# Unread identity products in PE's waits, and shorter chains in the norms, the router and the two tails

## What is computed

```python
for l in range(2):
    x_lat = x_lat + mod_l[2] * mixer(...)                 # layer 0 also for x_ctx
    h = _modulate(_rmsnorm(x_lat, norm_ffn[l]), mod_l[3], mod_l[4])
    # layer 0: 512 tokens (latent and context), layer 1: 256
    y = _hier_moe(tokens, ...)   # group = argmax of 4, then top 2 of its 8 experts, gates from a softmax
    x_lat = x_lat + mod_l[5] * y
return _rmsnorm(x_lat, final_norm)
```

## Time and profile before

| | |
|---|---|
| runs | median 2405.39 us, 2403.98 to 2409.56 us, 3 runs |
| the profiled execution | 2406.93 us, its span 2405.6 us |
| PE busy | 2192.5 us, 91% of the span |
| DVE, ACT, POOL busy | 657.5, 357.0, 121.5 us |
| DMA | 601.75 MB, mean 250 GB/s |
| mean granted clock of PE | 0.959 of full |

### The profile page before, as it was taken

The page is one execution under the profiler, slowest core; times in us unless marked ns, Lnnn a source line. Parts: engine busy times, 40 slices in busy tenths (PEclk is TensorE's granted clock), DMA queues, the critical chain, the costliest instruction groups (busy, mean ns, idle before and its releaser), DMA issues. The chain is left out here.

```text
span 2405.6 us, 27733 instructions
## 1 busy us (share of the span) xinstructions
PE 2192.5 (91%) x11542; PEld 1348.4 (56%) x11542; DVE 657.5 (27%) x1485; ACT 357.0 (15%) x831; POOL 121.5 (5%) x164
## 2 busy tenths in 40 slices
PE   6987998899999986999979999998599999989998
PEld 2454664656665543444555554544376458858873
DVE  2142332422222212313531111111355231034201
ACT  2052431200000001112520000000121122011000
POOL 4000000010000001000000000000110000000000
PEclk9988999899999998899989999999799999999999
DMA  9453163599999997621189999999644432443441
GB/s 331 143 216 136 56 260 149 209 414 420 420 420 420 421 420 295 225 71 67 50 322 415 420 419 420 419 420 418 229 142 134 133 112 97 158 140 119 153 152 41
DMA packets 154309, 601.75 MB, mean 250 GB/s; under 512 B 15289, under 2 KB 19073, under 8 KB 103488
## 3 DMA queue, kind: packets, MB, share of 16 engines
q1 hardware_dynamic: 144512, 582.98, 62.9%
q0 software_dynamic: 8144, 11.57, 1.5%
q10 hardware_dynamic: 1520, 5.32, 0.6%
HBM read 589.84 MB, written 21.23 MB: 254 GB/s over the span
## 5 line engine op out<-in xcount | busy, mean ns | idle before, releaser
L366 PE MATMUL psum<-ring,h_t 128*128 128x512 f32 (+1 forms) x1024 | 430.3, 582 | 4.5 <-ACT h_t L1072 2.1
L366 PEld LDWEIGHTS psum<-ring,h_t 128*128 128x128 f32 x1024 | 192.9, 193 | 234.8 <-issue 230.4
L399 PE MATMUL psum<-h_t,ring 128*128 128x256 f32 (+1 forms) x1424 | 311.7, 382 | 4.5 <-ACT ff_hid L2567 2.3
L399 PEld LDWEIGHTS psum<-h_t,ring 128*128 128x128 f32 (+1 forms) x1424 | 270.0, 190 | 45.9 <-issue 4.7
L2381 PE MATMUL psum<-ring,h_t 128*64 128x256 f32 x2272 | 262.1, 384 | 3.0 <-DMA ring<-in_expert_w_dram 2.1
L2381 PEld LDWEIGHTS psum<-ring,h_t 128*64 128x64 f32 x2272 | 158.0, 137 | 90.3 <-issue 11.8
L2381 PE MATMUL psum<-wide,h_t 128*64 128x256 f32 x1664 | 191.0, 382 | 2.3 <-DMA wide<-in_expert_w_dram 1.5
L2381 PEld LDWEIGHTS psum<-wide,h_t 128*64 128x64 f32 x1664 | 114.9, 137 | 66.6 <-issue 7.6
L337 DVE COPY h_t<-psum 128x512 f32<-128x512 f32 (+2 forms) x76 | 50.4, 663 | 319.6 <-PE psum L1933 294.5
L1933 PE MATMUL psum<-gates,h_row_tiles 128*128 128x256 f32 (+1 forms) x512 | 109.1, 370 | 5.6 <-DVE gates L1921 5.6
L1933 PEld LDWEIGHTS psum<-gates,h_row_tiles 128*128 128x128 f32 x512 | 89.9, 202 | 25.0 <-issue 12.2
(11 more groups left out here) (590 smaller groups left out, 2093.1 us busy)
## 6 DMA issues: line engine op xcount, KB each, us to landing
ring<-in_expert_w_dram SPq DMA_DIRECT2D x210, 1024.0 KB, 24.6
wide<-in_expert_w_dram SPq DMA_DIRECT2D x156, 1024.0 KB, 26.2
ring<-in_ada_w_dram SPq DMA_DIRECT2D x48, 1024.0 KB, 11.3
ring<-in_w_in_dram SPq DMA_DIRECT2D x30, 1024.0 KB, 5.1
ring<-in_diff_w_in_dram SPq DMA_DIRECT2D x12, 1024.0 KB, 15.7
gates<-in_expert_w_dram SPq DMA_DIRECT2D x12, 1024.0 KB
x<-in_expert_w_dram SPq DMA_DIRECT2D x12, 1024.0 KB, 27.8
ring<-in_w_gate_dram SPq DMA_DIRECT2D x12, 1024.0 KB, 4.9
```

The lines of the kernel that those rows point to most:

```text
L366: mm = k.nc.tensor.matmul(banks[r][0:m, 0:nn], lhs(k0 + j, r), w[:, j, :], start=(k0 + j == 0), stop=(k0 + j == k_tiles - 1))
L399: mm = k.nc.tensor.matmul(banks[i][0:h, 0:n_rhs], w[:, j, b:b + h], rhs(k0 + j), start=(k0 + j == 0), stop=(k0 + j == k_tiles - 1))
```

## The change

1. A helper `keep_going(k, bank, times, marks)`: PE waits for `marks`, then does `times` products of the identity with the identity spread over 512 columns, into PSUM bank 7. Nobody reads them. They are put in the norm before the router of both layers (three behind the wait for bank 7's last reader, two behind the reciprocal), in `first_tail` (two behind each of the first two tiles' addition), and in `second_tail` (two behind the landing of tile 0's results, three behind its product with `final_g`).
2. The gate copy on POOL is moved from before the norm to behind it.
3. `picks.select(0)` goes directly behind `at_slot`.
4. `between()` and `picks.select(1)` go ahead of the slot tables' copies on DVE, `select(1)` behind a wait for the last gathering product of group 0; it leaves `first_blocks`.
5. `first_tail` makes the first two tiles' scales before it adds tile 2's results; `second_tail` takes both tiles' roots at once, and scales and transposes after it.

```diff
+def keep_going(k, bank, times, marks=()):
+    pe = k.nc.tensor
+    wait_for(pe, marks)
+    for _ in range(times):
+        pe.matmul(k.psum[:, bank, :], k.ident[:], k.ident[:].unsqueeze(1).to_broadcast([P, 4, P]), start=True,
+                       stop=True)
@@ norm_to_columns
             ss, squared_at = squares
+            if wr is not None:
+                keep_going(k, 7, 3, [k.holder[7]] if k.holder and k.holder[7] else now(k.act_evac, k.dve_evac))
             rs = root_of_sums(k, ss, n, eps, squared_at)
+            if wr is not None:
+                keep_going(k, 7, 2, now(k.dve_step))
@@ second_tail
-        def root(i):
+        def roots():
+            t_all, v2_all, r_all = ss[:, 0:T_LAT, 0], ss[:, 0:T_LAT, 1], ss[:, T_LAT:2 * T_LAT, 0]
...
         add(0)
         times_g(0)
+        keep_going(k, 7, 2, now(loaded[0]))
+        keep_going(k, 7, 3, v_at[0])
...
-        root(0)
         times_g(1)
-        r_at = reciprocal(0)
...
-        for half in range(2):
-            scale(0, half, r_at)
-        root(1)
-        for kt in range(DK):
-            turn(0, kt)
-        r_at = reciprocal(1)
-        for half in range(2):
-            scale(1, half, r_at)
-        for kt in range(DK):
-            turn(1, kt)
+        r_at = roots()
+        for i in range(T_LAT):
+            for half in range(2):
+                scale(i, half, r_at)
+        for i in range(T_LAT):
+            for kt in range(DK):
+                turn(i, kt)
@@ route
+            chain(nc.vector, k.dve_step, nc.vector.scalar_tensor_tensor(
+                out=picks.at[:], in0=rank, scalar=1.0, in1=chosen[:, 0:n, :], op0=ALU.add, op1=ALU.mult))
+            picks.select(0)
...
-        picks.select(0)
...
+        between()
         picks.first_group(rows_at)
+        table_bank = k.psum[:, 5, :]
...
+        nc.vector.wait_ge(k.tensor_done.sem, picks.picked[0, 3])
+        picks.select(1)
+        wait_for(nc.tensor, ranked)
         picks.first_up()
-        wait_for(nc.tensor, told_at)
...
-        wait_for(nc.vector, now(k.tensor_done))
+        wait_for(nc.vector, slot_tables())
         k.dve_evac.mark(to_tables(table_bank))
@@ experts
-        k.behind("pool", k.stage())
-        for a in ffn_gates:
-            k.pool_step.mark(nc.gpsimd.tensor_copy(a[SLOT:P, 0:BANK], a[SLOT:P, BANK:D]))
-        gates_at = now(k.pool_step)
...
         norm_to_columns(k, f"ffn{l}", ...)
+        k.behind("pool", k.stage())
+        for a in ffn_gates:
+            k.pool_step.mark(nc.gpsimd.tensor_copy(a[SLOT:P, 0:BANK], a[SLOT:P, BANK:D]))
+        gates_at = now(k.pool_step)
...
-        between()
@@ first_tail
         squares(i)
+        keep_going(k, 7, 2, ([flow.holder[7]] if flow.holder[7] else []) + added[i])
+    parts = scaled_rows(0)
     add_pair(2)
-    turn(0, scaled_rows(0))
+    turn(0, parts)
@@ first_blocks
-        dve.wait_ge(*last_of(0))
-        picks.select(1)
```

More of the change, by code:

```diff
@@ L1162, in squares @@
             k.act_step.mark(nc.scalar.activation(junk[:], src, ACT.Square, scale=scale, accum_out=to))
-        def root(i):
+        def roots():
+            t_all, v2_all, r_all = ss[:, 0:T_LAT, 0], ss[:, 0:T_LAT, 1], ss[:, T_LAT:2 * T_LAT, 0]
             wait_for(dve, now(k.act_step, k.dve_step))
-            chain(dve, k.dve_step, nc.vector.tensor_scalar(t_of(i), t_of(i), 1.0 / D, eps, ALU.mult, ALU.add))
-            k.dve_step.mark(nc.vector.scalar_tensor_tensor(out=r_of(i), in0=t_of(i), scalar=eps, in1=v2_of(i),
+            chain(dve, k.dve_step, nc.vector.tensor_scalar(t_all, t_all, 1.0 / D, eps, ALU.mult, ALU.add))
+            k.dve_step.mark(nc.vector.scalar_tensor_tensor(out=r_all, in0=t_all, scalar=eps, in1=v2_all,
                                                            op0=ALU.mult, op1=ALU.add))
             wait_for(act, now(k.dve_step))
-            k.act_step.mark(nc.scalar.activation(r_of(i), r_of(i), ACT.Sqrt))
-        def reciprocal(i):
+            k.act_step.mark(nc.scalar.activation(r_all, r_all, ACT.Sqrt))
             wait_for(dve, now(k.act_step))
-            k.dve_step.mark(nc.vector.reciprocal(r_of(i), r_of(i)))
+            k.dve_step.mark(nc.vector.reciprocal(r_all, r_all))
             return now(k.dve_step)
@@ L1658, in scalar_phase, with route @@
     k.pump()
-def route(k, l, h_t, n_tiles, tables, rows, h_rows, gather_from, send_to, slot_w, control, n_blocks, picks, place_room, slot_w_lat):
+def route(k, l, h_t, n_tiles, tables, rows, h_rows, gather_from, send_to, slot_w, control, n_blocks, picks, place_room, slot_w_lat,
+          between):
     nc, sb = k.nc, k.sb
@@ L1803, in route @@
         nc.vector.wait_ge(k.dve_evac.sem, k.dve_evac.n)
-        picks.select(0)
+        ranked = now(k.dve_evac)
         def place(v):
@@ L1879, in route, with slot_tables @@
         control_at = (k.dve_step.sem, k.dve_step.n)
+        between()
         picks.first_group(rows_at)
-        picks.first_up()
-        wait_for(nc.tensor, told_at)
-        table_bank = k.psum[:, 5, :]
-        for mm in tokens_to_slots(nc.tensor, [table_bank]):
-            k.tensor_done.mark(mm)
-        wait_for(nc.vector, now(k.tensor_done))
+        table_bank = k.psum[:, 5, :]
+        def slot_tables():
+            wait_for(nc.tensor, told_at)
+            for mm in tokens_to_slots(nc.tensor, [table_bank]):
+                k.tensor_done.mark(mm)
+            return now(k.tensor_done)
+        nc.vector.wait_ge(k.tensor_done.sem, picks.picked[0, 3])
+        picks.select(1)
+        wait_for(nc.tensor, ranked)
+        picks.first_up()
+        wait_for(nc.vector, slot_tables())
         k.dve_evac.mark(to_tables(table_bank))
```

4 lines of the change are left out of this document (1 added, 3 removed).

## The result

The changed kernel took 2387.11 us, the median of 4 runs (2383.27 to 2389.78), against 2405.76 of the kernel before (4 runs): ratio 0.9924, interval 0.9899 to 0.9949. Over everything that was run, 30 runs of the changed kernel have a mean of 2386.7 us (scatter of one run 4.7) and 88 of the kernel before one of 2402.9 (5.3; run e5's single execution is not among them).

The account below looks back on a forecast made before the run. Late expert stages were taken as transfer-bound, their end set by when PE lets the weight stream start. Terms -7.1 (layer 0), -4.2 (layer 1), +1.5 and -0.6 (tails) gave -10.4 us: 2395.8 us, range 2389 to 2402.5.

Parts of the forecast that it names:

- the clock holds further: Rival: PE's clock stays high through the first group's gathering in both layers, some 4 us more gained, 2392; chance 0.15.
- what they buy is the clock ... -2.1: Layer 0's norm: unread products keep PE's clock up, so transposes and the four L595 run faster, -2.1 us.
- The gate copies at 0: Both norms: moving POOL's gate copies frees the squares' sum but delays the logits' copy equally, net 0.
- Select 0, -0.4: Layer 0's router: the first group's table, which PE waits for, is made earlier, -0.4 us.
- Select 1, -3.3 and -1.3: Layer 0, second group's table ahead of slot tables: -3.3 us of PE waiting, -1.3 from the clock staying up.
- Layer 1, -4.2: Sum of layer 1's norm, table and clock terms, -4.6 us, taken as -4.2 because the ring's first filling limits it.
- First tail, +1.5: Tail after layer 0: PE idles some 2.9 us before the q projection's weights and its clock falls, costing 1.5 us.
- Second tail, -0.6: Tail after layer 1: taking the roots together lets L399 start at 1726.4 rather than 1726.98, -0.6 us.
- What would show it: Expected trace signs: L480 0.2 us behind the squares, norm clock near 1.00, second-group wait under 1 us, L366 15 us or more.
- the clock isn't held: Rival: transposes don't keep PE's clock up, or it falls before the products; norm gains vanish, 2400.4 us; chance 0.15.
- Slower: Rival: the norm products run at 1.2 GHz and delay the transposes; in sum +5 us, 2411; chance 0.06.
- Transfers hide it all: Rival: bytes alone set the expert stages' end, so only the tails remain, +0.9 us, 2407.8; chance 0.07.

Follow-up runs that it names:

- e5: The kernel before, no edit, profiled once more: 2412.01 us in its one run.
- e13: The changed kernel without any unread products and with the gate copies ahead of the norm again: 2392.25 us (12 runs).
- e9: The changed kernel, products kept, with only the gate copies put ahead of the norm again: 2384.48 us (6 runs).
- e4: The changed kernel with the second group's table made behind the slot tables again, as before the change: 2396.79 us (12 runs).

## Why the prediction was wrong

The direction, the places and the terms that stood in the sum held. What the sum put at nothing did not: PE's clock behind the norm.

- *The step that failed* is the rival "the clock holds further", kept out of the sum at a chance of 0.15. The term in the sum, "what they buy is the clock ... -2.1", was right. From the first of the norm's transposes to the last product with the router's weights PE took 10.54 us without products and 8.54 with them, the gate copies ahead of the norm in both (runs e13, e9): -2.0. But behind the router layer 0 gained 1.1 us in the count (0.54 + 0.97 against 0.90 + 1.75) and 2.9 in the gathering (7.38 against 10.26), and these 4.0 us are what its start gained beyond the forecast (-6.6 against -2.5). The rival had priced the gathering at 2.7. In layer 1 it didn't come: the gathering there became slower (below).
- *What brought these 4.0 us*: 1.4 of the gathering came with the earlier select 0 (below). The count's 1.1 and the other 1.4 came with the products or with the moved copies, either being enough; the 1.4 failed to come in three traces of eleven. Of the 4.9 us that products and moved copies give together (37.25 to 32.4), the products alone give 4.5 and the copies alone 3.7. How the moved copies do it alone, beyond the 0.3 of waiting, stays open.
- *The gate copies at 0*: right as a sum of waits (0.3). I had counted their 1.7 us gap behind the logits against the rival; it measured 1.3 (PE waits 2.06 instead of 0.75 us) and doesn't decide: with products, count and gathering were fast without the gap too (run e9).
- *Select 0, -0.4*: the wait is -0.4; with the clock of the gathering behind it -1.8.
- *Select 1, -3.3 and -1.3*: -5.5. PE's reading of the control word, charged with 0.6, left no gap on PE at all.
- *Layer 1, -4.2*: -6.7. Select 1 gave 1.8, where 1.0 was forecast, and the second projection 1.7, as forecast, though not safely by select 1 (run e4 kept it with the wait back). The norm's clock gave 2.0, where 1.8 were forecast (7.04 us without products, 5.02 with them), at the forecast price of 0.2. Yet up to first_up only 1.0 of 1.9 was gained, since from the first gathering to first_up it took 6.5 to 7.1 us instead of 5.8, more of it at the low clock. Another 2.2 us came in the 450 us behind the second projection. That stretch took 461.1 and 462.0 us before, 457.2 to 458.1 in the changed kernel, and 456.9 to 460.3 in others with the same start (457.4 with select 1 alone); what makes it differ wasn't isolated. After the 4.0 us it is the largest part of the miss, and it has no cause here. That the ring would take 0.4 back didn't show.
- *First tail, +1.5*: +2.1, and with the wait of 2.9 us right (3.11), but the cause was only half seen: the price is there without products in two traces of three (L366 16.05 and 15.83 us, the third 13.97). The "3 to 6 us" of low clock that priced it don't stand in rows 11, which have 0.50 over all of 10 us. That L366 then lost 1.4 to 3.0 us, as such a stretch would, was luck.
- *Second tail, -0.6*: -0.9. From the landing of tile 0's results to L399 it took 15.6 us before and 14.5 to 14.7 in the seven traces without products there, so the gain is the order's; with products it took 13.4 to 15.0.
- *What would show it*: the signs appeared, L480 at 0.30, ACT's idle time of 2.96 released by POOL, no gap ahead of the second group, L366 at 15.4 to 17.0. The granted clock in this window over layer 0's norm, third number from the right:

```profile
400.00:414.00 14.00, 12.66 (x58) 6.50 (x58) 7.11 (x16) 7.47 (x15) 0.00 (x0) 1.00 0.95 363
```

It is 1.00, and 32 of the 58 instructions in it are transposes: with that *the clock isn't held* falls. The clock also rose among transposes alone, the 32 of L1734 (418.08 to 423.46): it is 0.50 from 419 to 422, 0.94 from 422 to 423 and 1.00 behind. The Trainium skill (TensorE: Matmul & The Clock Gate, PE-mode transpose) says that a transpose doesn't count as PE being busy in the same way; these windows show no effect of that. *Slower* fell too: the norms' products took 0.46 us an instruction in layer 0 and 0.50 at most in layer 1; only the second tail's first four ran at 0.90. *Transfers hide it all* falls by the table: the long stage kept its length.

## What to carry to other kernels

Find where PE's clock is low between the start of a stage and its first long stretch, and ask of each such place whether another engine covers it. Filling PE's waits is worth what the uncovered work behind them gains, which can lie far behind the filling: price it there too. A shorter wait is worth less than its length if the low stretch then falls on uncovered work. Take two edits that may serve the same end away singly and together, since either may do alone. Where executions scatter by more than an edit is worth, compare stages that begin where the edit begins, in several traces: one stage here had two forms, 1.4 us apart, in the same code.

## What the hardware showed that I had not expected

The low clock behaves like a stretch of time that is spent somewhere, not like a property of an instruction group: with the same instructions ahead, it lay on the transposes (5.38, then 7.38 for the gathering) or on the gathering (3.71, then 8.81), in kernels whose code up to there is the same. Waits of 1.1 to 3.5 us ahead of L366 were followed by a low clock in ten traces of eleven, unless filled; of two alike, 1.12 us was (15.83) and 1.19 us wasn't (13.97); one of 0.54 us was so in one execution (L366 16.12 us), one of 0.49 us wasn't (13.97). In the norm, five unread products of 0.91 us each cost the chain nothing in layer 0 and 0.2 us in layer 1, as forecast.
